# The first mixer of a two-block forward pass: Toeplitz transfers, the copy of V, scaled keys, state copies and weight rounding in another order

## What is computed

```python
h = rms_norm(x, mix_pre_g[l])
proj = h @ w_mix_in[l]
q, k, v, u = jnp.split(proj, [ATTN_WIDTH, 2 * ATTN_WIDTH, 3 * ATTN_WIDTH], axis=-1)
attn = dilated_attention(q, k, v)          # 8 heads of 64
ssm = s5_mixer(u, a_re, a_im, log_dt, b_re, b_im, c_re, c_im, d_skip, w_glu, b_glu)
mixed = jnp.concatenate([attn, ssm], axis=-1) @ w_mix_out[l]
x = x + rms_norm(mixed, mix_post_g[l])
...
# s5_mixer, per group of 16 channels: x_t = a_bar x_(t-1) + B_bar u_t, y_t = Re(C x_t) + d u_t
y = jax.nn.gelu(y.reshape(B, S, SSM_WIDTH))
return y * jax.nn.sigmoid(y @ w_glu.astype(f32) + b_glu.astype(f32))
```

## Time and profile before

| | us |
|---|---|
| median of 3 runs | 2904.72 (2904.3 to 2906.03) |
| the profiled execution | 2909.29 |
| its span in the profile | 2907.5 |
| mean granted clock of TensorE | 0.993 |
| the mixer from the end of v to the output matrix | about 444 to 569 |

### The profile page before, as it was taken

How to read it: one execution, slowest core, us unless ns; L and a number is a source line. 1 busy time by engine, 2 the same in 40 slices (tenths; PEclk the granted TensorE clock), 3 DMA queues, 4 the chain that set the end, 5 groups by cost and what they waited for, 6 DMA issues and landing times.

```text
span 2907.5 us, 34562 instructions
## 1 busy us (share of the span) xinstructions
PE 2859.6 (98%) x14616; PEld 2361.9 (81%) x14616; DVE 1232.1 (42%) x1695; ACT 1011.7 (35%) x1400; POOL 391.2 (13%) x420
## 2 busy tenths in 40 slices
PE   9999999899999999999999999999999999999998
PEld 7888886578888888888878888888888888788886
DVE  5554343453433433334657333343332465633333
ACT  5232344653322333223434322234322343433222
POOL 0115617101110000010131000100001013200010
PEclk9999999899999999999999999999999999999999
DMA  4333223023333233332222333323333222233332
GB/s 148 102 94 95 94 80 88 25 87 93 96 95 102 87 94 99 98 95 86 82 60 79 96 100 94 94 87 95 99 97 94 86 84 64 73 98 98 94 94 80
DMA packets 77322, 262.12 MB, mean 90 GB/s; under 512 B 12208, under 2 KB 12336, under 8 KB 77168
## 3 DMA queue, kind: packets, MB, share of 16 engines
q1 hardware_dynamic: 77168, 259.91, 29.5%
HBM read 256.60 MB, written 2.10 MB: 89 GB/s over the span
## 4 chain that ended last, share of the span: by engine, by line
PE 94%; DVE 2%; ACT 2%; issue 1%; SPq 1%; POOL 0%; DMA 0%; DVEq 0%; POOLq 0%; ACTq 0%
PE bank L336 25%; PE bank L338 25%; PE bank L337 25%; PE bank L353 2%; PE bank L359 2%; PE bank L354 2%; PE bank L473 2%; PE bank L402 1%; PE bank L406 1%; PE bank L403 1%; PE bank L484 1%; SPq L2222 1%; PE bank L369 1%; PE bank L368 1%; PE bank L373 1%
## 5 line engine op out<-in xcount | busy, mean ns | idle before, releaser
L1363 DVE TENSOR_TENSOR wlo<-wraw,whi 128x1024 fp32r<-128x1024 f32 x474 | 594.7, 1266 | 868.5 <-ACT whi L856 867.7
L856 ACT ACTIVATE whi<-wraw 128x1024 fp32r<-128x1024 f32 x479 | 500.5, 1055 | 943.6 <-DMA wraw<-weights 942.6
L336 PE MATMUL bank<-Hh,whi 128*128 128x512 f32 x2104 | 821.6, 390 | 3.0 <-DVE wlo L1363 2.3
L338 PE MATMUL bank<-Hl,whi 128*128 128x512 f32 x2104 | 818.8, 389 | 0.0
L337 PE MATMUL bank<-Hh,wlo 128*128 128x512 f32 x2104 | 818.7, 389 | 0.0
L336 PEld LDWEIGHTS bank<-Hh,whi 128*128 128x128 f32 x2104 | 395.0, 188 | 85.1 <-DVE wlo L1363 2.2
L338 PEld LDWEIGHTS bank<-Hl,whi 128*128 128x128 f32 x2104 | 394.9, 188 | 82.5
L337 PEld LDWEIGHTS bank<-Hh,wlo 128*128 128x128 f32 x2104 | 395.1, 188 | 81.6 <-issue 0.3
L336 PE MATMUL bank<-Ah,whi 128*128 128x512 f32 x1056 | 412.5, 391 | 0.0
L338 PE MATMUL bank<-Al,whi 128*128 128x512 f32 x1056 | 411.0, 389 | 0.0
L337 PE MATMUL bank<-Ah,wlo 128*128 128x512 f32 x1056 | 410.8, 389 | 0.0
(11 more groups left out here) (300 smaller groups left out, 2624.3 us busy)
## 6 DMA issues: line engine op xcount, KB each, us to landing
wraw<-weights SPq DMA_DIRECT2D x479, 512.0 KB, 3.6
X<-x_t SPq DMA_DIRECT2D x8, 256.0 KB, 6.6
y_t<-X SPq DMA_DIRECT2D x8, 256.0 KB, 2.0
dist<-attention SPq DMA_DIRECT2D x4, 256.0 KB, 3.4
Y<-masks SPq DMA_DIRECT2D x1, 512.0 KB, 8.8
zsum<-attention SPq DMA_DIRECT2D x2, 256.0 KB, 4.2
MUb<-attention SPq DMA_DIRECT2D x2, 256.0 KB, 4.4
MUb<-ssm SPq DMA_DIRECT2D x1, 256.0 KB, 8.0
```

Of the source, the lines that this page charges most:

```text
L336: pe.matmul(b, sh, mh, start=start, stop=False)
L338: signal(pe.matmul(b, sh, ml, start=False, stop=stop), keys)
L856: act.activation(whi[:, u % NS, :], wraw[:, u % NS, :], ACT.Copy).then_inc(*S.done("weights_hi", ("hi", u)))
L1363: dve.tensor_tensor(wlo[:, u % NS, :], wraw[:, u % NS, :], f32(whi[:, u % NS, :]), SUB).then_inc(*S.done("weights_lo", ("lo", u)))
```

## The change

It moves work within the first mixer. No arithmetic changes.

- **SyncE.** The 32 Toeplitz transfers become `toeplitz(0, 1)`, four of them ahead of load 83 as before, and `toeplitz(1, 8)`, 28 behind load 83 and the distances 4 and 5, ahead of load 84.
- **Scalar.** V is copied ahead of `inputs(2)` and `inputs(3)`. The two state copies are gone. The state products' evictions come at iterations 13 and 15 (were 11 and 15), and the rounding of units 84 and 85 behind gelu (was iteration 12).
- **Vector.** `scaled("qk1")` is in two parts, one ahead of iteration 5, one behind iteration 6. The state copies are behind iteration 9 (were behind 7), the evictions of state products behind 11 and 14 (were 9 and 13), the remainders of 84 and 85 behind gelu's.
- **GpSimd** makes the two state copies right behind the recurrence.
- **TensorE.** `ssm` runs in iterations 10 to 13 one part each, in 14 and 15 two. Banks 1 and 3 of `qk1` stay held until iteration 6, so the banks from iteration 8 on are others.

```diff
@@ TensorE
-                    pe.wait_ge(*S.at(("XS2 act", 1)))
+                    pe.wait_ge(*S.at(("XS2 pool", 1)))
...
-            gemm_group("qk1", None, (("H free", "m1"),), lambda k: next(heads), 0, (Mh, Ml))
+            gemm_group("qk1", None, (("H free", "m1"),), lambda k: next(heads), 0, (Mh, Ml), True)
+            B.let_go(("qk1", 0)), B.let_go(("qk1", 2))
             for d in heads:
-                if d > 7:
-                    ssm((d - 8) // 2, d % 2)
+                if d == 6:
+                    B.let_go(("qk1", 1)), B.let_go(("qk1", 3))
+                if 9 < d < 14:
+                    ssm((d - 10) // 2, d % 2)
+                if d > 13:
+                    ssm(d - 12, 0)
+                    ssm(d - 12, 1)
@@ Scalar
-                if d == 7:
-                    act.wait_ge(*S.at("recurrence"))
-                    for g2 in range(2):
-                        act.activation(XS2[64 * g2:64 * g2 + 64, :, g2:32:2], XS[64 * g2:64 * g2 + 64, :, g2, :],
-                                       ACT.Copy).then_inc(*S.done("s5_act", ("XS2 act", g2)))
...
-                if d in (11, 15):
-                    ssm((d - 8) // 2)
-                if d == 12:
-                    hi_to(p + 15)
+                if d in (13, 15):
+                    ssm(d - 12)
@@ Vector
-            scaled("qk1", 2)
+                if k == KD - 1:
+                    scaled("qk1", 2, (0,))
...
-                if d == 7:
+                if d == 6:
+                    scaled("qk1", 2, (1,))
+                if d == 9:
                     dve.wait_ge(*S.at("recurrence"))
...
-                if d in (9, 13):
-                    ssm((d - 8) // 2)
-                if d == 12:
-                    lo_to(p0 + 15)
+                if d == 11:
+                    ssm(0)
+                if d == 14:
+                    ssm(2)
@@ GpSimd
+            for g2 in range(2):
+                pool.tensor_copy(XS2[64 * g2:64 * g2 + 64, :, g2:32:2], XS[64 * g2:64 * g2 + 64, :, g2, :]).then_inc(
+                    *S.done("s5_pool", ("XS2 pool", g2)))
+                pool.wait_ge(*S.at(("XS2 pool", g2)))
@@ SyncE
-                for m in range(8):
-                    for q in range(4):
-                        sp.dma_start(W3[16 * m:16 * m + 16, 8 * q:8 * q + 8, 16 * m:P],
-                                     Kr[32 * q:32 * q + 16, :, 0:P - 16 * m]).then_inc(skip_in, 16)
+                toeplitz(0, 1)
             if u == at_m1 + 14:
                 sp.wait_ge(*S.at(("score", 6)))
                 distances(4)
                 sp.wait_ge(*S.at(("score", 7)))
                 distances(5)
+                toeplitz(1, 8)
```

More of the change, by code:

```diff
@@ L1108, in mixer_1 @@
                     turn_u(k - 1)
+                if k == KD - 1:
+                    act.wait_ge(*S.at(("full", "v")))
+                    for m in range(4):
+                        act.activation(Vt[:, m, :], bank(("v", m))[:, :], ACT.Copy, scale=rcol[:, m:m + 1]).then_inc(
+                            *S.done("s5_act", ("Vt", m), empties=[("v", m)]))
                 if k > 5:
@@ L1111, in mixer_1 @@
                     inputs(2 * k - 11)
-            act.wait_ge(*S.at(("full", "v")))
-            for m in range(4):
-                act.activation(Vt[:, m, :], bank(("v", m))[:, :], ACT.Copy, scale=rcol[:, m:m + 1]).then_inc(
-                    *S.done("s5_act", ("Vt", m), empties=[("v", m)]))
             for k in range(KD):
@@ L1199, in mixer_1 @@
                 act.activation(yh[:, cb, :], yg[:, cb, :], ACT.Copy).then_inc(*S.done("moving_hi", ("yh", cb)))
+            hi_to(p + 15)
             for nb in range(4):
@@ L1725, in mixer_1, with scaled @@
                 lo_to(START["m1"] + 64 + 4 * k + 3)
-            def scaled(use, hb):
+            def scaled(use, hb, parts=(0, 1)):
                 dve.wait_ge(*S.at(("full", use)))
                 dve.wait_ge(*S.at(("Rb", "m1")))
-                for i in range(2):
+                for i in parts:
                     dve.scalar_tensor_tensor(Qf[:, hb + i, :], bank((use, i))[:, :], 0.125, Rb[:, :], MUL, MUL).then_inc(
@@ L1825, in mixer_1 @@
                     *S.done("moving_lo", ("yl", cb)))
+            lo_to(p0 + 15)
             for nb in range(4):
@@ L2190, in distances, with toeplitz @@
             sp.dma_start(dist[h % 4][:, :], att_d[:, h, :]).then_inc(dist_in[h % 4], 16)
+        def toeplitz(m0, m1):
+            for m in range(m0, m1):
+                for q in range(4):
+                    sp.dma_start(W3[16 * m:16 * m + 16, 8 * q:8 * q + 8, 16 * m:P],
+                                 Kr[32 * q:32 * q + 16, :, 0:P - 16 * m]).then_inc(skip_in, 16)
         load(0)
```

## The result

| | before | changed |
|---|---|---|
| median of four runs each, us | 2905.38 (2904.3 to 2908.12) | 2889.28 (2887.36 to 2889.51) |
| the profiled execution, us | 2909.29 | 2887.36 |
| its span, us | 2907.5 | 2885.6 |
| mean granted clock | 0.993 | 0.997 |
| start of the mixer's output rows, us | 568.95 | 546.82 |

The medians lie 16.1 us apart, a ratio of 0.9945, where 19.3 us were forecast. The ratio on record is 0.9939 with a 95% interval of 0.9926 to 0.9951, that is, 14.2 to 21.5 us less. The time lies 3.9 us above the forecast of 2885.4 and inside its range. The two profiled executions differ by more, 21.9 us. From the start of the output rows to the end of the span both take the same, 2338.6 and 2338.8 us, so in these two executions all of it is won in the first mixer.

The account below looks back on a forecast made before the run. TensorE, busy 98% of the span, was taken as the bound, with GpSimd later at the state products. Output rows at 525.2 + 24.5 = 549.7 instead of 568.95, -19.3 us, gave 2890.0 profiled, 2885.4 median; range 2880 to 2893.

Parts of the forecast that it names:

- Steps 1 and 2: First mixer: V copied before inputs 2 and 3, -4.4 us; 28 Toeplitz transfers put behind load 83, -7.2 us.
- step 5: First state product to the mixer's output rows: 24.5 us instead of 35.6, later weight rounding and a new half clock included.
- Some 7 us: Length of the 1.2 GHz stretch after each TensorE wait of about 2 us or more, wasting 0.46 us per busy microsecond.
- Step 3: Keys and queries scaled by heads: the wait for Kf goes, a new one of 1 to 2 us comes, -1 us.
- Step 4: State copies on GpSimd, state products two iterations later: first one at 525.2 us, TensorE waiting 2 to 3 us for it.
- The gain so far meets a time that doesn't move: At the state products: GpSimd's recurrence ends near 520.5 us whatever TensorE does, and its copies follow.
- Step 6: Weights 84 and 85 rounded behind gelu: costs nothing, with 0.9 us of cover; at most 2 us without it.
- GpSimd becomes the bound: Rival: GpSimd's state copies slower than any row, or Vector shut out; gain 12 to 16 us, 2889 to 2893; chance 0.12.
- It doesn't do what it says: Rival: load 83 stays late, so step 2's gain is lost; about 14 us remain, 2891; chance 0.04.
- Clock stays up: Rival: wait ahead of state products under 2 us, no half clock follows; gain 22 to 24 us, 2881 to 2883; chance 0.14.
- given back later: Rival: weights 84 and 85, gelu's bank or state evictions cost more; gain 6 to 12 us, 2893 to 2899; chance 0.07.
- slower: Rival: GpSimd's pair of copies takes over 23 us, so the first state product starts after 544.5; chance 0.03.

Follow-up runs that it names:

- a_again: The changed kernel run once more, unaltered, as base of its group: 2889.55 us, ratio 0.9939 to the kernel before.
- a_pool_thrice: The changed kernel with GpSimd's pair of state copies made three times over: 2896.98 us, ratio 0.9966 to the kernel before.
- c_gelu_bank: The changed kernel with the bank of values 3 not handed to gelu's first pair: 2887.01 us, ratio 0.9929 to the kernel before.
- a_act_copies: The changed kernel with the two state copies back on Scalar, behind iteration 9: 2891.97 us, ratio 0.9948 to the kernel before.
- x_weights: The kernel before with only the rounding of units 84 and 85 moved behind gelu: 2903.23 us, ratio 0.9986.
- x_transfers: The kernel before with only 28 of the 32 Toeplitz transfers moved behind load 83: 2901.90 us, ratio 0.9979.
- x_states: The kernel before with only state copies on GpSimd and state products two iterations later: 2905.24 us, ratio 0.9992.

## Why the prediction came out as it did

- **Steps 1 and 2** held in mechanism and place. The waits of 1.99 and 4.0 and their stretches are gone; `qk1` ends at 504.8 for "near 505". Alone they brought 3.3 for 4.4 and 5.2 for 7.2, and step 5's weights 3.8 for 6.8. The term that was too high for a part by itself is the half clock, as far as the runs can tell: by the mean clocks 1.8 for 2.4, 0.9 for 3.2, and 1.8 for step 5's 3.2, each uncertain by 1.5, so that only step 2's is clearly too high. "Some 7 us" was read from one execution; such a wait is followed by 3, 7 or 10 us, or by none, and while other long waits stay, half clock turns up behind those. All together it was not too high: the prediction's clock terms sum to -7.6 (2.4, 3.2, 3.2 and 0.8, less 2.0), and a_again has 17.8 us less half clock, give or take 4, which at 0.27 to 0.46 is 4.8 to 8.2 us.
- **Step 3**: -1 forecast, 1.3 measured, with the new wait for Qf of 1.22 in the 1 to 2 us given.
- **Step 4** failed in what it says of the path, though its point in time is near. By its own sign ("wrong if TensorE gets to the state products after GpSimd is done") it is wrong: GpSimd was done at 522.4, TensorE got there at 523.8. "The gain so far meets a time that doesn't move" is not what the traces show. GpSimd had 1.2 us of slack (a_pool_thrice), and the pair that ends last is Vector's. It starts right behind Vector's scores of iteration 9, which follow TensorE, and not behind the recurrence: that had ended 1.5 us before it in the changed kernel, and 0.3 before it in c_gelu_bank, where the two came closest. What GpSimd does cost here is that Vector's copies take longer beside its own: the pair was stretched by 0.8 (2.20 for 1.41), in c_gelu_bank by 1.5 (2.89), for +1.0. The single terms: the recurrence ended at 520.0 for 520.5; GpSimd's copies took 1.17 us each for 1.8, within 0.88 to 2.93 and near the lower end. The sentence "TensorE waits 2 to 3 us for it" failed too. TensorE came without the wait, because 3.4 us at half clock, behind the wait of 2.06 for `Ml`, cost it some 1.6 us just ahead of this point. The prediction knew that wait ("about 2") and put its clock behind the state product. In c_gelu_bank it was so.
- **Step 5**: 23.0 us for 24.5. The items came as listed: 0.42 at scores 28 for 0.5, 1.22 at iteration 13 for 1.0, 1.48 at gelu for 1.5. The new half clock of +2.0 was absent, for the reason just given.
- **Step 6** cost nothing, as forecast.
- **The sum.** In the traces the output rows moved by 22.1 us for 19.3, the profiled time is 2887.4 for 2890.0. The medians moved by 16.1, and by 17.6 in the next group; both intervals take in 19.3. That the forecast's level lies 3.9 us below the median is the last step's doing, and it would be further off if the sum had not erred the other way, which is luck: "the median of the runs lies 4.6 below it", carried over to the changed kernel. There the profiled execution lies 1.9 below the median instead, an error of 6.5 against the 2.6 gained in the sum. The distance is no constant, since it depends on how much half clock the profiled execution happened to have: over the whole span 42.6 us in the trace of before, 16.9 in the one after, 25.7 less (11.8 us of time), where the mean clocks of a_again's group give 17.8 less (8.2 at most). With the 10.6 us of waits that is 22.4 for the traces (21.9 measured), and at most 18.8 for the runs (17.6).
- **The rivals.** The measured 2889.3 lies at the upper bound of the sum (2889.6) and also in the range of "GpSimd becomes the bound" (2889 to 2893), so the time alone doesn't tell the two apart. The traces do: the copies were faster than taken, not slower, and GpSimd had slack, so this rival is out. "It doesn't do what it says" (2891) is out too, with load 83 issued at 483.11. "Clock stays up" gives the 22 us between the profiled executions, for another reason: the wait ahead of the state products wasn't there at all. Nothing in the runs speaks for "given back later" or "slower". (The 24.3 us in the latter is the 24.5 of step 5; nothing hangs on it.)

The two places that the prediction drew on. The trace agrees with the lock (the Trainium skill, SBUF — State Buffer, "Who interferes with whom"): Vector's pair takes 1.41 us without GpSimd's copies beside it and 2.17 to 3.08 with them. The estimate of 1.54 us a copy (the Trainium skill, GPSIMD Engine Reference, "3.1 Elementwise — side-by-side cycle accounting") was too high; the measurement, 1.17 us, decides.

## What to carry to other kernels

Where a wait is followed by a stretch at half clock, count the wait in full, but the clock's share with a wide range, and less than one trace shows while other long waits stay: singly, parts that were reckoned at 4.4, 7.2, 5 and 6.8 us brought 3.3, 5.2, 1.8 and 3.8. Before moving a step so that an engine arrives earlier, look for the engine that does not move with it, and test its slack by doing its work several times over. Then compare how far its end moved with how far the waiting instruction moved: the difference is the slack, and it can be there though the stretched kernel is slower. And don't carry a profiled execution's distance to the median over to another kernel: compare the clocks of the runs instead.

## What the runs showed of the chip

- The same wait, 2.06 us at the same instruction, was followed by 3.4 us at 1.2 GHz in both traces of the changed kernel and in a_pool_thrice, by 6.8 in a_act_copies and by none in c_gelu_bank, whose TensorE programs are the same up to there. The wait of 1.99 us for V was followed by 6.8 us in three traces (before twice, x_weights) and by 3.4 in two (x_transfers, x_states). The wait of 1.8 us near 2482 was followed by 3.4 us in one trace of the kernel before and by none in the other.
- This goes with most of the spread of a kernel whose program does the same in every run: 2904.5 us at a mean clock of 0.995, 2910.7 at 0.991.
- GpSimd copies 1024 float32 elements in each of 64 partitions, with a stride in what it writes, in 1.09 to 1.15 us, 1.1 ns an element, nearer to its memset (0.86) than to its two-input operation (2.86). Beside Vector's copies one took 1.46 to 1.48. The copies of the tile in c_gelu_bank (duration in ns, min/median/max), where the two engines ran side by side:

```profile
L2126 POOL COPY XS<-XS x2: 1145/1304/1462, 521.6 to 522.8; 64x1024 f32<-64x1024 f32 x2
L1820 DVE COPY XS<-XS x2: 1366/1428/1490, 521.9 to 523.3; 64x1024 f32<-64x1024 f32 x2
```
